# A hybrid decoder step: the first token chunk projected before its RMS root, with DMAs requeued and a second pair of PSUM banks for turned probabilities

## The reference

```python
h = x * rsqrt(mean(x * x) + 1e-6) * norm_g
z = h @ w_in                       # columns of four mixers and of their gates
A: forgetting attention, 4 heads x 64 (paged K, V and log-forget cache for samples)
B: RWKV-7 time mixing, 4 heads x 64, matrix state and token shift
C: causal pooling over 2/4/8/16 tokens    D: GLU, depthwise width 31, LayerNorm, swish, pointwise
x = x + concat(A*silu(gA), B*silu(gB), C*silu(gC), D*silu(gD)) @ w_out
y = rmsnorm(x, final_norm_g)       # also returned: k, v, logf, the final states
```

## Time and profile before

| | |
|---|---|
| median of 3 runs | 1932.46 us (1923.53 to 1933.47) |
| the profiled execution | 1928.07 us, span 1926.3 us |
| PE busy | 1773.4 us, 92% |
| DVE busy | 776.4 us, 40% |
| ACT busy | 477.7 us, 25% |
| POOL busy | 174.9 us, 9% |
| mean granted TensorE clock | 0.962 of 2.4 GHz |

### The profile page before, as it was taken

How to read it: one execution, slowest core, us unless ns; L and a number is a source line. 1 busy time by engine, 2 the same in 40 slices (tenths; PEclk the granted TensorE clock), 3 DMA queues, 4 the chain that set the end, 5 groups by cost and what they waited for, 6 DMA issues and landing times.

```text
span 1926.3 us, 35542 instructions
## 1 busy us (share of the span) xinstructions
PE 1773.4 (92%) x15076; PEld 1094.4 (57%) x15076; DVE 776.4 (40%) x1640; ACT 477.7 (25%) x855; POOL 174.9 (9%) x220
## 2 busy tenths in 40 slices
PE   6999999999999999299697999998989878999997
PEld 3555555555554555286464677788878743444442
DVE  3450699742221541311553554435545551112112
ACT  4301100010327231002343454422222270000000
POOL 1000000011000003720000000000000002111210
PEclk9999999999999999699798999999999978999998
DMA  6223320376312345231565324467655267788782
GB/s 228 78 84 106 121 88 34 135 191 164 118 67 89 132 166 190 85 122 27 169 197 134 98 86 141 145 208 227 187 153 155 91 260 290 275 298 272 273 290 72
DMA packets 154512, 300.77 MB, mean 156 GB/s; under 512 B 20285, under 2 KB 124589, under 8 KB 136238
## 3 DMA queue, kind: packets, MB, share of 16 engines
q1 hardware_dynamic: 131746, 154.72, 25.8%
q0 software_dynamic: 18240, 115.82, 17.6%
q10 hardware_dynamic: 4368, 27.96, 3.6%
HBM read 236.73 MB, written 63.96 MB: 156 GB/s over the span
## 4 chain that ended last, share of the span: by engine, by line
PE 71%; DVE 13%; DMA 6%; ACT 4%; issue 3%; SPq 2%; another core or an unknown queue 1%; POOL 0%; ACTq 0%; DVEq 0%
PE psum L795 22%; PE psum L1051 13%; PE psum L1341 13%; DVE big L1733 8%; PE psum L988 6%; PE psum L1014 3%; PE psum L881 3%; PE psum L1001 3%; PE psum L975 2%; DMA big<-zsD 2%; ACT big L1410 2%; PE psum L775 2%; PE psum L827 1%; DMA rkv<-big 1%; DMA big<-zT 1%
## 5 line engine op out<-in xcount | busy, mean ns | idle before, releaser
L795 PE MATMUL psum<-big,wbuf 128*128 128x416 f32 x1920 | 675.8, 513 | 5.6 <-DVE big L1663 3.4
L795 PEld LDWEIGHTS psum<-big,wbuf 128*128 128x128 f32 x1920 | 364.9, 190 | 311.9 <-issue 310.2
L1051 PE MATMUL psum<-big 64*64 64x64 f32 (+3 forms) x5792 | 218.6, 263 | 25.3 <-issue 12.1
L1051 PEld LDWEIGHTS psum<-big 64*64 64x64 f32 (+2 forms) x5792 | 165.1, 132 | 87.8 <-issue 53.7
L1379 ACT ACTIVATE zst<-psum 128x416 f32<-128x416 f32 x125 | 64.0, 517 | 539.1 <-PE psum L795 539.0
L1341 PE MATMUL psum<-big 128*128 128x512 f32 (+1 forms) x408 | 186.5, 607 | 1.1 <-issue 1.1
L757 POOL DMA_INDIRECT big<-in_cache_v,pidx x64 | 60.6, 947 | 986.5 <-PE psum L1014 684.6
L1733 DVE SCALAR_TENSOR_TENSOR big<-big,pars 128x2048 f32<-128x2048 f32 x120 | 148.2, 1298 | 1.1
L1341 PEld LDWEIGHTS psum<-big 128*128 128x128 f32 (+1 forms) x408 | 73.5, 187 | 97.6 <-issue 97.6
L2175 DVE TENSOR_TENSOR zst<-zst,psum 128x1024 f32<-128x1024 f32 (+1 forms) x17 | 20.7, 1220 | 229.6 <-PE psum L1341 229.6
L1641 ACT ACTIVATE big<-zst 128x1024 f32<-128x1024 f32 (+1 forms) x17 | 18.0, 1057 | 301.1 <-DVE zst L2175 301.1
(11 more groups left out here) (240 smaller groups left out, 1839.4 us busy)
## 6 DMA issues: line engine op xcount, KB each, us to landing
big<-in_k_pages SPq DMA_DIRECT2D x432, 128.0 KB, 2.3
zT<-zst ACTq DMA_DIRECT2D x25, 1040.0 KB, 6.7
wbuf<-in_w_slots SPq DMA_DIRECT2D x24, 512.0 KB, 4.7
big<-zT POOLq DMA_DIRECT2D x11, 1024.0 KB, 5.6
zst<-in_k_pages SPq DMA_DIRECT2D x80, 128.0 KB, 2.5
rwS<-big POOLq DMA_DIRECT2D x8, 1024.0 KB, 4.2
big<-rwS SPq DMA_DIRECT2D x8, 1024.0 KB, 5.8
zst<-in_x_prompt SPq DMA_DIRECT2D x16, 512.0 KB, 8.5
```

The lines of the kernel that those rows point to most:

```text
L795: last = nc.tensor.matmul(psum[:, m % CHUNKS, 0:CW], w[:, k, :], hT[:, k, c * CW:(c + 1) * CW], start=(k == 0), stop=(k == KT - 1))
L1051: return nc.tensor.matmul(out, l, r, start=start, stop=stop, skip_group_check=True)
```

## The change

1. Start: DVE writes x_raw = x * norm_g for chunk 0 as soon as x and norm_g (now in a DMA of its own) are there, and slots 0 and 1 project x_raw. The root is multiplied on by DVE as it takes these two results from PSUM. hT of chunk 0, which slots 2 and on use, is made last, from x_raw. Squares of chunk 0 are all on ACT, and their sum over k is three DVE adds like the other chunks'.
2. SP issues the state and the v_rows ahead of wvf, masks and aux. POOL's gathers wait for the four v_rows too.
3. The outputs of k, v, logf and shift move from SP (at j = 11) to POOL, behind the 64 gathers and after 12 finished items.
4. turn_probs takes banks 6, 7 and 4, 5 in turn, and waits for the copies of the block before the last.

Semaphore counts follow. The diff, cut to its core:

```diff
+        rs_raw = area(PO + 4 * CW, CW)
...
+        x_raw = area(SA, KT, CW)
...
+        raw_ready = sem("raw_ready")
+        raw_scaled = sem("raw_scaled")
...
+            sp.wait_ge(v_spread, 16 * DEC_SEQ)
+            sp.dma_start(s_wkv[0], I['state_T']).then_inc(s_in, 16)
+            for i in range(DEC_SEQ):
+                sp.dma_start(v_row[i], zsD[i].unsqueeze(1).to_broadcast([2, 64, 1024])).then_inc(x_in[i], 16)
             sp.dma_start(wvf, I['w_vf']).then_inc(pars_in, 16)
...
             sp.dma_start(aux[:, :], I['aux']).then_inc(rows_in, 16)
-            sp.wait_ge(v_spread, 16 * DEC_SEQ)
-            sp.dma_start(s_wkv[0], I['state_T']).then_inc(s_in, 16)
-            for i in range(DEC_SEQ):
-                sp.dma_start(v_row[i], zsD[i].unsqueeze(1).to_broadcast([2, 64, 1024])).then_inc(x_in[i], 16)
...
-                if j == 11:
-                    for t in range(2):
-                        sp.dma_start(O['kT'][t], zT[KA + t]).then_inc(st_stored, 16)
-                    sp.wait_ge(vf_evac, TT + 1)
-                    sp.dma_start(O['v_prompt'][0, 0].rearrange("(n p) h d -> p n (h d)", p=P), vtok[:, 0:TT, 0:256]).then_inc(st_stored, 16)
-                    sp.dma_start(O['v_sample'].rearrange("b l t h d -> (b l t) (h d)"), vtok[0:SMP, TT, 0:256]).then_inc(st_stored, 16)
-                    sp.wait_ge(nl_ready, 2)
-                    sp.dma_start(O['logf_prompt'][0, 0].rearrange("(n p) h -> p n h", p=P), lo[:, 0:TT, :]).then_inc(st_stored, 16)
-                    sp.dma_start(O['logf_sample'].rearrange("b l t h -> (b l t) h"), lo[0:SMP, TT, :]).then_inc(st_stored, 16)
-                    sp.dma_start(O['shiftE'], zT[R0:R0 + 7, :, SEQ - 1:T_ALL]).then_inc(st_stored, 16)
...
             pool.wait_ge(idx_ready, 1)
+            for i in range(DEC_SEQ):
+                pool.wait_ge(x_in[i], X_SEEN[i] + 16)
...
                 gather(scores_[:, x:x + PAGE], cf, lidx[:, t:t + 1], lf_in)
+            pool.wait_ge(o_read, 12)
+            for t in range(2):
+                pool.dma_start(O['kT'][t], zT[KA + t]).then_inc(st_stored, 16)
+            pool.wait_ge(vf_evac, TT + 1)
+            pool.dma_start(O['v_prompt'][0, 0].rearrange("(n p) h d -> p n (h d)", p=P), vtok[:, 0:TT, 0:256]).then_inc(st_stored, 16)
+            pool.dma_start(O['v_sample'].rearrange("b l t h d -> (b l t) (h d)"), vtok[0:SMP, TT, 0:256]).then_inc(st_stored, 16)
+            pool.wait_ge(nl_ready, 2)
+            pool.dma_start(O['logf_prompt'][0, 0].rearrange("(n p) h -> p n h", p=P), lo[:, 0:TT, :]).then_inc(st_stored, 16)
+            pool.dma_start(O['logf_sample'].rearrange("b l t h -> (b l t) h"), lo[0:SMP, TT, :]).then_inc(st_stored, 16)
+            pool.dma_start(O['shiftE'], zT[R0:R0 + 7, :, SEQ - 1:T_ALL]).then_inc(st_stored, 16)
...
+                elif m in (CHUNKS, CHUNKS + 1):
+                    pe.wait_ge(raw_scaled, m - CHUNKS + 1)
...
-                    pe.wait_ge(z_evac, m - CHUNKS + 1)
+                    pe.wait_ge(z_evac, m - CHUNKS - 1)
                 for k in range(KT):
-                    if n == 0:
-                        pe.wait_ge(hT_ready, KT * c + k + 1)
-                    last = nc.tensor.matmul(psum[:, m % CHUNKS, 0:CW], w[:, k, :], hT[:, k, c * CW:(c + 1) * CW], start=(k == 0), stop=(k == KT - 1))
+                    if n < 2 and c == 0:
+                        pe.wait_ge(raw_ready, k + 1)
+                        x = x_raw[:, k, :]
+                    else:
+                        if n == 0:
+                            pe.wait_ge(hT_ready, KT * (c - 1) + k + 1)
+                        elif n == 2 and c == 0:
+                            pe.wait_ge(hT_ready, KT * (CHUNKS - 1) + k + 1)
+                        x = hT[:, k, c * CW:(c + 1) * CW]
+                    last = nc.tensor.matmul(psum[:, m % CHUNKS, 0:CW], w[:, k, :], x, start=(k == 0), stop=(k == KT - 1))
...
             def square_sums(c):
-                if c > 0:
-                    pe.wait_ge(ssum_ready, c)
-                    nc.tensor.matmul(psum[:, 5 + c % 3, 0:CW], ones_ln[:, :], ssum[:, c % 2, :], start=True, stop=True).then_inc(ss_mm, 1)
-                    return
-                pe.wait_ge(made, EPS)
-                for n, k in enumerate((0, 4, 1, 5, 2, 6, 3, 7)):
-                    if k < 4:
-                        pe.wait_ge(sqx, k + 1)
-                    else:
-                        pe.wait_ge(sqd, k - 3)
-                    last = nc.tensor.matmul(psum[:, 5, 0:CW], ones_ln[:, :], sq_x[:, 0, k, :], start=(n == 0), stop=(n == KT - 1))
-                last.then_inc(ss_mm, 1)
+                if c == 0:
+                    pe.wait_ge(made, EPS)
+                pe.wait_ge(ssum_ready, c + 1)
+                nc.tensor.matmul(psum[:, 5 + c % 3, 0:CW], ones_ln[:, :], ssum[:, c % 2, :], start=True, stop=True).then_inc(ss_mm, 1)
...
-            square_sums(0)
             for c in range(CHUNKS):
                 chunk(0, c)
+                if c == 0:
+                    square_sums(0)
                 if c + 1 < CHUNKS:
                     square_sums(c + 1)
...
                 if blk == 0:
...
-                else:
-                    pe.wait_ge(D['pT'], D0['pT'] + 2 * blk)
+                elif blk >= 2:
+                    pe.wait_ge(D['pT'], D0['pT'] + 2 * (blk - 1))
...
-                    last = transpose(psum[:, 6 + j // 4, (j % 4) * P:(j % 4 + 1) * P], rows[:, TJ - 1 - j, :])
+                    last = transpose(psum[:, 6 - 2 * (blk % 2) + j // 4, (j % 4) * P:(j % 4 + 1) * P], rows[:, TJ - 1 - j, :])
...
-            act.dma_start(pars[:, :], I['pars']).then_inc(pars_in, 16)
+            act.dma_start(pars[:, 84:99], I['pars'][:, 84:99]).then_inc(rows_in, 16)
+            act.dma_start(pars[:, 0:84], I['pars'][:, 0:84]).then_inc(pars_in, 16)
+            act.dma_start(pars[:, 99:], I['pars'][:, 99:]).then_inc(pars_in, 16)
...
             def chunk(n, c):
...
+                done[0] += 1
+                if m < 2:
+                    return
...
-                done[0] += 1
...
-                    act.wait_ge(z_evac, m + 1)
+                    act.wait_ge(z_evac, m - 1)
+                    if n < 2:
+                        act.wait_ge(raw_scaled, n + 1)
...
             def squares(c):
...
-                if c == 0:
-                    for k in range(4):
-                        a_(sq_x[:, 0, k, :], hT[:, k, 0:CW], ACT.Square, sqx)
-                    return
-                if c == 2:
-                    act.wait_ge(ss_mm, 1)
-                if c > 2:
-                    act.wait_ge(ssum_ready, c - 2)
+                if c >= 2:
+                    act.wait_ge(ssum_ready, c - 1)
...
             def inverse_root(c):
...
-                if c >= 2:
-                    act.wait_ge(hT_ready, KT * (c - 1))
-                a_(rs[:, c % 2, :], psum[:, 5 + c % 3, 0:CW], ACT.Ln, rs_ready, scale=256.0 / D_MODEL, bias=rms_eps)
+                to = rs_raw if c == 0 else rs[:, c % 2, :]
+                if c >= 3:
+                    act.wait_ge(hT_ready, KT * (c - 2))
+                a_(to, psum[:, 5 + c % 3, 0:CW], ACT.Ln, rs_ready, scale=256.0 / D_MODEL, bias=rms_eps)
...
-                a_(rs[:, c % 2, :], rs[:, c % 2, :], ACT.Exp, rs_ready, scale=-0.5)
+                a_(to, to, ACT.Exp, rs_ready, scale=-0.5)
...
             squares(0)
+            squares(1)
             inverse_root(0)
-            squares(1)
             for c in range(CHUNKS):
                 chunk(0, c)
                 if c + 1 < CHUNKS:
...
-                    nc.scalar.copy(scores_[:, x:x + 512], psum[:, 6 + hf, :]).then_inc(D['pT'], 1)
+                    nc.scalar.copy(scores_[:, x:x + 512], psum[:, 6 - 2 * (blk % 2) + hf, :]).then_inc(D['pT'], 1)
...
-            for k in range(4, KT):
-                v.tensor_tensor(sq_x[:, 0, k, :], hT[:, k, 0:CW], hT[:, k, 0:CW], ALU.mult).then_inc(sqd, 1)
-            dve.wait_ge(pars_in, 16)
-            for c in range(CHUNKS):
-                cs = slice(c * CW, (c + 1) * CW)
+            dve.wait_ge(rows_in, 16)
+            for k in range(KT):
+                v.tensor_scalar(x_raw[:, k, :], hT[:, k, 0:CW], par7[:, k:k + 1], None, ALU.mult).then_inc(raw_ready, 1)
...
+            def square_tree(c):
+                dve.wait_ge(sqx, c + 1)
+                q = sq_x[:, c % 2]
+                ch.link(v.tensor_tensor(q[:, 0:4], q[:, 0:4], q[:, 4:8], ALU.add))
+                ch.link(v.tensor_tensor(q[:, 0:2], q[:, 0:2], q[:, 2:4], ALU.add))
+                if c >= 2:
+                    dve.wait_ge(ss_mm, c - 1)
+                v.tensor_tensor(ssum[:, c % 2, :], q[:, 0], q[:, 1], ALU.add).then_inc(ssum_ready, 1)
...
+            def normed(c):
                 dve.wait_ge(rs_ready, 2 * c + 2)
                 for k in range(KT):
-                    v.scalar_tensor_tensor(hT[:, k, cs], hT[:, k, cs], par7[:, k:k + 1], rs[:, c % 2, :], ALU.mult, ALU.mult).then_inc(hT_ready, 1)
```

(34 more changed lines are left out.)

## The result

The changed kernel took 1911.4 us (median of 12 runs, 1906.5 to 1918.7), the kernel before 1923.4 (12 runs, 1914.1 to 1933.5, among them the three known before, whose median was 1932.5). The ratio is 0.9933, its 95% interval 0.9914 to 0.9952, so 12.9 us were won (9 to 17). I had forecast 31.8 us and 1898. That lies in the range I gave, but the gain is less than half of what I worked out. The profiled execution of the changed kernel took 1912.0 us (span 1910.0), 16.3 less in span than that of before.

What follows compares the result with a forecast made beforehand. PE was taken to bound the kernel, carrying 71% of its chain of waits. 5.8 + 0.8 + 15.0 + 10.2 = 31.8 us off the profiled 1928.1 gave 1896.3; with runs averaging 1929.8 it said 1898, range 1884 to 1914.

Steps and rivals of the forecast that it cites:

- outputs on POOL: At item 14, SP freed of the outputs issues key pages earlier, so PE stops waiting: 15.0 us won, bounds 17.5 and 3.
- I take off 1.5: At item 14, 1.5 us deducted from 16.5 because the outputs' 4.43 MB now move at the same time as the key pages.
- POOL's issues trickle: At item 14, the sign held against outputs and key pages colliding on the DMA engines; no size given.
- The start: First projections: PE begins chunk(0, 0) at 10.6 and reaches slot 2 at 79.9 instead of 85.7, 5.8 us won; bounds +8 and 0.
- The state loads: Sample state: last v_row at 790.3, but aux behind it at 793.8 holds DVE's casts; 0.8 us won, bounds +8 and -4.
- The term that I called eaten: Sample state: +8 us if aux does not queue behind the v_rows; the edit's own order was said to eat this gain.
- Turned probabilities: End phase: two pairs of banks bring blocks from 3.2 us to ACT's 1.1; 10.2 us won, bounds 5.5 and 12.
- (a): Item 14: outputs and key pages collide on the DMA engines, giving 3 us instead of 15, time 1910; chance 0.12.
- (b): Start: gives nothing, as three pauses each cost a stretch at the low clock; time 1904; chance 0.12 together with (e).
- (c): Sample state: aux does not queue behind the v_rows; time 1891; chance 0.08.
- (e): End phase: PE stays at the low clock despite the second pair of banks; time 1903; chance 0.12 together with (b).
- (d): Key steps from item 14 on all wait because POOL's queue moves outputs slowly; slower than before, 1935 and more; chance 0.03.

## Why the prediction was right or wrong

**The failed step: outputs on POOL, 15.0 us.** The table gives 38.4 on average for the four traces with the outputs on SP ahead of the pages, and 36.4 for the five with them on POOL at the twelfth item: 2.0 us. The two groups overlap (36.7 to 39.5 and 35.7 to 37.9), and the time of the kernel with only this part, at a ratio of 0.9999, tells no gain; so 2.0 is an estimate from traces, which no time confirms. What I said of SP held: the pages' issue began at 997.5, as far ahead as the step before allowed. What failed is "I take off 1.5" for the collision. I had read that 4.43 MB took 76% of all engines for 20 us, and named the bound, 3 us, if the pages land as late as the outputs' traffic makes them. Then I let "POOL's issues trickle" speak against it. They do not: POOL had issued all seven within 5.3 us, and 4.41 MB of its queue then lay on the same engines as 2.1 MB of pages, and these took SP 17.1 us to issue. With the outputs elsewhere (22.8 us for the same stretch) the full gain is 15.5 us against before; I had priced it at 16.5 less the collision. So the delay was there and its size was right, and the edit moved it from SP's queue to the DMA engines. The rule of the Trainium skill that I had weighed ("DMA: Bandwidth & Descriptors", Issuing engines are not separate DMA queues: all issuers share the 16 engines, and a second one saves only the time of issuing) says this, and the runs agree with it: 2.0 us by a new issuer, 15.5 by a new place.

**The start, 5.8 us.** The steps were near: scaled x at 10.2 (9.9), PE at 10.8 (10.6), 8.86 for the first chunk (8.8), 1.24, 1.57 and 0.63 of waits (1.3, 1.9 and 0.6). Wrong was chunk(1, 0). The pause ahead of it was 2.85 and not 2.3, as chunk 1's squares ended at 19.5 and its adds at 23.1, and behind it 7.19 us went by instead of 5.6. I had this as a bound ("if each pause costs a stretch at the low clock") and not in the sum. It was one pause of the four, the longest. Seven traces with this start have slot 2 at 83.0 on average against 85.7 for four with the old one, 2.7 us; and at the first gate product 1.6 are left of it (925.1 for four traces of the changed start and state, 926.7 for three of before). The start alone measured no gain (0.9979 to 1.0013). One loss on the way shows in the traces: behind the pause near 607 PE took 12.16 us in three of the four traces with the old start and 13.85 or more in all ten with a new one; but the fourth, with the old start, took 13.84, so this cannot be put down to the start.

**The state loads, 0.8 us.** Right in kind and size. The last v_row no longer decided, aux did. Against the trace of before, whose stores of the second half of the RWKV inputs begin 4.0 us later (715.7 and 711.7), I expected the casts at 789.8 (793.8 less 4.0) and the second step at 800.9 (804.9 less 4.0); they came at 790.4 and 801.1. SP's order gained nothing by itself. The term that I called eaten, +8, is what the kernel with aux first showed on PE, 8.3 us. And the reading that a v_row is bound by two engines was the most valuable one of the case: with all engines, and aux first, the whole wait of 38 us is gone. By the Trainium skill's rule on the slowest dimension (same page, Why a DMA increments its semaphore by 16) 64 rows in place of 2 use all engines, and the eight DMAs agree: 82.1% of the engines in place of 12.4%.

**Turned probabilities, 10.2 us.** Right: the end phase is 74.2 us on average in four traces without and 64.4 in the ten with the second pair of banks, 9.8 us. In the trace of the changed kernel two blocks took 2.4 us, 1.2 each (1.1 said), and PE had the high clock. The value tile's wait of 5.9 us for its gather is at the upper end of the ten traces with this edit (3.4 to 6.1).

**The sum.** 1.6 (start and state together) + 2.0 + 9.8 = 13.4 us, against 12.9 measured. The pair of profiled executions shows 16.3: 2.9 us more, which is less than what traces of one stretch differ by: the RWKV stretch goes from 268 to 281 us over the traces, without a change in it. I also set the forecast on 1929.8, the mean of three runs; the median of twelve is 1923.4. That the measured time lies in my range is luck of this base: 6.4 us lower, the same sum and bounds give 1892 and a range of 1878 to 1908, which does not hold 1911.4.

**The rivals.** (a) is what happened at item 14, 3 us said and 2.0 measured; I gave it 0.12. Its 1910 against 1911.4 is in part luck: by its own sum, 19.8 us, 1923.4 becomes 1903.6, and the 6.9 us that the gain fell short of this sum and the base's 6.4 made up for each other. (b) is true in part: one pause ran into the low clock, and 1.6 of 5.8 us were left. (c) and (e) did not come, (d) neither: no early key step after item 14 was late in any kernel with the outputs at the twelfth item (57.6 throughout). Two kernels show the nearest thing to it, 6.8 us for one later step.

## What to carry to other kernels

In this case the bytes decided, and not the issuer. Before a store is moved to another queue, add up the bytes that will be in flight together with the load that waits: if the engines are busy for longer than the load's slack, the store has to go to another time, not to another issuer. A row that shows a queue at 12.4% of 16 engines, so at two of them, was worth more here than the order of the queue: 41 us at the first gate product by width and aux first, nothing that could be told by the order. And where PE is made to start earlier, put short independent work where it would pause: here that won 5 us at slot 2.

## What the hardware did that I had not expected

- The issue of sixteen DMAs of 128 KB took SP 8.1 to 9.7 us at all other steps of the changed kernel and of the one before, and 13.1, 15.8 and 17.1 us with 4.4 MB of others in flight. So, in these traces, a late landing showed first as a long issue.
- A later start was a faster one, in one execution: 2.7 us later at the first projection, 1.8 us earlier at slot 2. The chunk behind the pause of 1.20 us ran at a granted clock of 1.00, the stretch behind that of 2.85 us at 0.78.
- The same pause of 2.95 us near 607 was followed by 34 matmuls that took 12.16 us in three traces and 13.84 to 15.15 in eleven; of two kernels with the same start, in which it ended 0.3 us apart, one is on either side. The time behind such a pause could not be foretold here to 2 us from one trace.
